# A recurrence of sixteen chains: two chains in turn over shifted periods, or one chain over one whole period

## The chip, the cores and the metric

One core of a Trainium2 chip. The metric is the time of one execution on the device in microseconds. The kernel before was run three times. One further execution was profiled; its span and its own time are given below.

## What is computed

One layer of a trunk for 128 context tokens and 512 latent tokens, width 2048, all in 32-bit floats. Its parts are a modulation, one input projection, three parallel token mixers, one output projection and a mixture of 16 experts. The change touches one of the mixers alone, the bidirectional recurrence (RWKV-7) of 16 heads of 64. The reference, cut to it:

```python
def wkv_scan(r, w, k, v, a, b, s0, reverse):
    def step(S, xs):
        r_t, w_t, k_t, v_t, a_t, b_t = xs
        sa = jnp.einsum('bhvk,bhk->bhv', S, a_t)
        S = S * w_t[:, :, None, :] + sa[..., None] * b_t[:, :, None, :] + v_t[..., None] * k_t[:, :, None, :]
        return S, jnp.einsum('bhvk,bhk->bhv', S, r_t)
    xs = tuple(jnp.swapaxes(t, 0, 1) for t in (r, w, k, v, a, b))
    s_T, o = lax.scan(step, s0.astype(jnp.float32), xs, reverse=reverse)
    return jnp.swapaxes(o, 0, 1), s_T

# one scan for each direction d, with its own decay and rate;
# the outputs of the two directions are added
o_d, s_d = wkv_scan(rf, decay_d, k_d, vf, -kk, kk * a_d, s0_d, rev)
o = outs[0] + outs[1]
```

The latent tokens start from a cached state, the context tokens from zero, and the final state of the context is an output of its own.

## The kernel before, in words

The program is a row of blocks, one after another: modulation, input projection, keys and attention, the recurrence (`block_rwkv`, lines 1112 to 1780), its output, output projection with experts, and a last block. Only `block_rwkv` is changed.

**Chains.** Heads are handled in pairs, 128 partitions for two heads; eight pairs and two directions make 16 chains, v = 0 to 15, pair v // 2 and direction v % 2. The 640 tokens are cut into 10 chunks of 64 (2 of context, 8 of latent). Within a chunk everything is matrix products; from chunk to chunk a state of 64 x 64 a head is carried. So each chain has parallel work, which is done for all its chunks at once, and a serial part of 10 chunks.

**The parallel work of a chain**, as jobs of PE into a ring of four PSUM banks (`rw_rot`, line 1491), each emptied by ACT or DVE. A job waits until the job four before it is emptied.
- w and a (four jobs) and s0: low-rank projections to decay and rate, and the turned start state. ACT empties them with tanh (lines 1579, 1581, 1583). After w, POOL shifts (line 1350), DVE makes the running sum (`scan`, line 1705), POOL makes products (`front`, lines 1358 to 1368), ACT exponentials (line 1613), DVE and POOL the scaled operands (lines 1710, 1717, 1722, 1372).
- sc, five jobs: the scores between tokens of a chunk, masked by DVE (line 1685).
- bk, three jobs, and vt, two jobs for each pair (in even periods): keys and values turned to rows (ACT, lines 1588, 1585).
- The inverse of a triangular matrix for each chunk. Blocks of 8 are sent over DRAM (SP, lines 1298 and 1301), solved by POOL (`solve`, lines 1395 to 1398), sent back (lines 1306, 1308) and laid out by `place` (line 1408). Then three levels (2, 3, 4), each with two x jobs and two d jobs; DVE empties x (line 1692) and d (line 1695) and transposes (`turn`, line 1677), which the next x job needs. The last d goes into `rw_tw` (line 1700), and `spread_own` (POOL, line 1415) fills its other half. `half0`, `half1` and `far` are copies of scores by ACT (line 1598).

**The serial part.** For each chunk three stages in this order (`stage`, lines 1503 to 1547 for PE):
- `pw`: five products with the values, the scores and the old state (rw_zo, rw_wu). It waits for the state of the chunk before and for the copy of its output. ACT copies the result to `rw_wsb` (line 1633).
- `u`: one product with the inverse; ACT copies to `rw_usb` (line 1641).
- `z`: two products; DVE makes the new state `rw_st` (line 1748, in the first chunk line 1746), and after it ACT copies the output to `rw_of` (line 1648).

**The order.** It is written out by hand in a list for each period u, `LINES[u]`. PE, ACT and DVE all walk through the same list and take what is theirs, in this order and no other. In a period u stand: the front jobs of chain u + 1, scores and bk of chain u, the levels of chain u - 1, and stages of chains. `spread_out` puts the stages, in equal measure, where the list says "slot". POOL and SP have orders of their own (loops from lines 1432 and 1314). In the kernel before the stages of a chain are shifted over parts of periods by `CUTS`: chunks 0 and 1 of chain v in the late part of period v + 1, chunks 2 to 4 in the early part of period v + 2, 5 and 6 in its late part, 7 to 9 in the early part of v + 3. `both` lets two chains take turns, stage by stage. There are 19 periods:

```python
return (spread_out(early(u), both(chain(u - 3, c, NCK), chain(u - 2, a, b)))
        + spread_out(late(u), both(chain(u - 2, b, c), chain(u - 1, 0, a))))
```

Of the kernel before, what the change touches and what calls it, by code (L numbers as in the profile page):

```python
# [20 lines left out]
P = 128  # L21
# [5 lines left out]
GRID_W, NAH, DH = 64, 8, 64  # L27
# [5 lines left out]
NCK = T // CK  # L33
# [1094 lines left out]
def block_rwkv(nc, z_d, kk_d, par_d, w2, a2, state, ident_d, o_raw_d, state_out, ffn_d, lb_d, tb_d, consts):  # L1128
# [9 lines left out]
    LEVELS = range(FIRST_LV, LAST_LV + 1)  # L1138
    CUTS = (2, 5, 7)
    STEPS = 2 * (SB - 2)  # L1140
# [7 lines left out]

    def early(u):

        w0, w1, a0, a1, s0 = front_jobs(u + 1) or [None] * 5
        now = u < NU
        sc = [("sc", b, u) if now else None for b in range(NCK // 2)]
        bk = [("bk", b, u) if now else None for b in range(2)]
        lv = {(kind, b, n): (kind, b, n, u - 1) if 1 <= u <= NU else None for kind in ("x", "d") for b in range(2) for n in LEVELS}
        turns = ["turn0", "turn1"] if 1 <= u <= NU else []
        items = [w0, a0, w1, a1, s0, "slot", sc[0], "scan", "slot", sc[1], "slot", sc[2], "slot", sc[3], "slot", sc[4], *turns, lv["x", 0, 2], "slot", lv["x", 1, 2], "slot", "removal",
                 lv["d", 0, 2], lv["d", 1, 2], "slot", "exp_in", lv["x", 0, 3], "slot", bk[0], lv["x", 1, 3], "exp_inv", "slot", "pad_b", lv["d", 0, 3], "slot", "half0",
                 lv["d", 1, 3], "exp_ex", "slot", "half1", "pad_k", lv["x", 0, 4], "slot", "decay", bk[1], lv["x", 1, 4], "slot", "far", lv["d", 0, 4], "slot", "pad_a", lv["d", 1, 4]]
        return kept_items(u, items)  # L1160

    def late(u):

        now = u < NU
        vt = [("vt", b, u) if now and u % 2 == 0 else None for b in range(2)]
        return kept_items(u, ["slot", ("bk", 2, u) if now else None, "slot", vt[0], "slot", vt[1], "slot"])

# [7 lines left out]
    def chain(v, i0, i1):  # L1175
        return [("seq", v, i, s) for i in range(i0, i1) for s in ("pw", "u", "z")] if 0 <= v < NU else []

    def both(one, two):
        return [s for pair in itertools.zip_longest(one, two) for s in pair if s is not None]

# [13 lines left out]
    def timeline(u):  # L1194

        a, b, c = CUTS
        return (spread_out(early(u), both(chain(u - 3, c, NCK), chain(u - 2, a, b)))
                + spread_out(late(u), both(chain(u - 2, b, c), chain(u - 1, 0, a))))

# [5 lines left out]

    LINES = [timeline(u) for u in range(NU + 3)]
    JOBS = front_jobs(0) + [i for line in LINES for i in line if not isinstance(i, str) and i[0] != "seq"]
# [7 lines left out]
    with ExitStack() as ctx:  # L1215
# [17 lines left out]
        bktok = sb("bktok", [P, NS, 2 * NCK, DH])  # L1233
        vtok = sb("vtok", [P, 2, NCK, DH])
        sc = sb("sc", [P, NS, NCK, 2, 2 * CK])
# [38 lines left out]
        def _(sp):  # L1274
# [10 lines left out]

            def store(p):
                for d in range(2):
                    sp.wait_ge(w_ev[d], p * NCK + NCP + 1)
                    sp.dma_start(state_out[d, bass.ds(2 * p, 2)].rearrange("o v k -> (o v) k"), fo[:, (2 * p + d) % 4, :]).then_inc(fo_out, 16)
                sp.wait_ge(osum_done, p + 2)  # L1290
                sp.dma_start(o_raw_d[bass.ds(p, 1)].rearrange("o p t -> p (o t)"), osum[:]).then_inc(o_out, 16)
# [49 lines left out]
        def _(pool):  # L1341
# [86 lines left out]
            for u in range(NU + 3):  # L1428
                if u + 1 < NU:
                    shift(u + 1)  # L1430
                if 1 <= u <= NU:
                    place(u - 1)
                if u + 1 < NU:
                    front(u + 1)
                    scaled_r(u + 1)
                if 1 <= u <= NU:
                    for b in range(2):
                        spread_own(u - 1, b)
                if u < NU:
                    solve(u)  # L1440
                if u + 1 < NU:
                    decay_pairs(u + 1)
                if u % 2 == 0 and 0 <= u // 2 - 2:
                    add_directions(u // 2 - 2)


        @block.tensor
        def _(pe):
# [64 lines left out]
            def stage(v, i, s):  # L1513
# [5 lines left out]
                wv, uv, fv, zv, ov = w[:, 0:DH], w[:, DH:2 * DH], w[:, 2 * DH:3 * DH], z[:, 0:DH], z[:, DH:2 * DH]  # L1519
                vk = vtok[:, v // 2 % 2, c, :]  # L1520
                if s == "pw":
# [41 lines left out]
        def _(act):  # L1563
# [3 lines left out]
            def empty(key):  # L1567
# [12 lines left out]
                elif kind == "a":  # L1580
                    a = nc.scalar.activation(ar[:, cols], bank[:, 0:HALF], ACT.Tanh, scale=0.5, bias=pp[:, 7 + u % 2:8 + u % 2])
                elif kind == "s0":
                    a = nc.scalar.copy(s0[:, u % 4, :], bank[:, 0:DH])
                elif kind == "vt":
                    a = nc.scalar.copy(chunks(vtok[:, u // 2 % 2], b).rearrange("p c k -> p (c k)"), bank[:, 0:BC * DH])
                elif kind == "bk":
                    m = min(8, 2 * NCK - 8 * b)
                    a = nc.scalar.copy(bktok[:, u % NS, 8 * b:8 * b + m, :].rearrange("p c k -> p (c k)"), bank[:, 0:m * DH])
# [1129 lines left out]
```

## Time and profile before

| what | us |
|---|---|
| median of three runs (3059.43 to 3063.23) | 3063.07 |
| the profiled execution, its own time | 3060.63 |
| its span | 3058.9 |
| PE busy, share of the span | 2697.3, 88% |
| DVE busy | 1367.3, 45% |
| ACT busy | 521.8, 17% |
| POOL busy | 453.7, 15% |
| first PE record of the recurrence | 1006.3 |
| its last output copy on ACT | 1526.1 |

The span is that of one execution in the hardware profile. Times of rows are microseconds from its start. PE is the matmul engine, PEld its loading of weights, SPq the queue of DMA issues. A product of two heads in 32-bit floats shows as four PE records. A row of the timeline merges records of the same kind; its second number is from the start of the first to the end of the last, and ends of matmuls overlap with what follows. PEclk is the granted clock of PE as a share of 2.4 GHz.

### The profile page before, as it was taken

The numbers are of one execution on the slowest core, as the hardware profiler recorded it, in microseconds if no ns is written. First come the engines' busy times: TensorE is split into PE (matmuls) and PEld (weight loads), VectorE is DVE, ScalarE is ACT, GpSimd is POOL, SyncE is SP. The second block draws the span as 40 slices with busy tenths as digits, with TensorE's granted clock in tenths as the row PEclk, the third lists the DMA queues.
The fourth block names the chain that finished last, engine by engine and source line by source line (L and its number), as shares of the span: only waits on it lengthen the run. The fifth ranks groups of instructions, "written<-read, shape, count | busy, mean of one in ns | idle before, by whom it ended". The sixth has DMA issues, their size and how long they took to land. (4 is left out here: it accounts for less than half of the span.)

```text
span 3058.9 us, 60845 instructions
## 1 busy us (share of the span) xinstructions
PE 2697.3 (88%) x25988; PEld 1525.7 (50%) x25988; DVE 1367.3 (45%) x2369; ACT 521.8 (17%) x1459; POOL 453.7 (15%) x639
## 2 busy tenths in 40 slices
PE   5799899999949489999867999999999999999992
PEld 1466676666637388888733444322333333333320
DVE  1658667676456355555371213432222333222323
ACT  1100000000045245555320211100000000000001
POOL 0100000000074455555120000000000000000000
PEclk8899999999979699999878999999999999999996
DMA  9576654646275311211078788899999999999997
GB/s 409 199 235 190 203 175 177 218 169 218 73 217 114 132 40 43 69 42 44 24 260 286 288 288 324 305 414 385 405 404 403 404 404 387 402 405 406 404 413 269
DMA packets 268517, 783.60 MB, mean 256 GB/s; under 512 B 99473, under 2 KB 163112, under 8 KB 199712
## 3 DMA queue, kind: packets, MB, share of 16 engines
q1 hardware_dynamic: 257104, 724.13, 63.0%
q0 software_dynamic: 10848, 56.51, 6.3%
q8 instruction: 152, 2.49, 0.3%
q14 instruction: 45, 0.37, 0.0%
q10 hardware_dynamic: 368, 0.10, 0.0%
HBM read 712.59 MB, written 68.08 MB: 255 GB/s over the span
## 5 line engine op out<-in xcount | busy, mean ns | idle before, releaser
L2207 PE MATMUL oe_ps<-experts_ring,tail_arena 128*32 128x512 f32 x4096 | 502.7, 606 | 43.7 <-DMA experts_ring<-in_w_up 43.7
L478 DVE SCALAR_TENSOR_TENSOR pj_macc<-pj_mring,head_cond_t,pj_macc 128x1024 f32<-128x1024 f32 x240 | 296.8, 1277 | 183.3 <-DMA pj_mring<-in_w_ada 183.3
L2207 PEld LDWEIGHTS oe_ps<-experts_ring,tail_arena 128*32 128x32 f32 x4096 | 149.3, 112 | 344.1 <-issue 343.1
L551 PE MATMUL pj_ps<-head_hT,head_ring_in 128*128 128x320 f32 x1104 | 312.4, 436 | 6.5 <-DVE head_hT L451 4.2
L2240 PE MATMUL oe_ps<-experts_ring,oe_hidt 128*32 128x512 f32 x2880 | 312.0, 592 | 0.0
L2215 PE MATMUL oe_ps<-experts_ring,tail_arena 128*32 128x512 f32 x2048 | 271.2, 597 | 0.0
L551 PEld LDWEIGHTS pj_ps<-head_hT,head_ring_in 128*128 128x128 f32 x1104 | 210.9, 191 | 96.7 <-DVE head_hT L451 6.6
L2544 DVE SCALAR_TENSOR_TENSOR oe_hid_s<-oe_hid_s,oe_gcol_s,oe_ps 128x512 f32<-128x512 f32 x16 | 12.0, 747 | 536.3 <-ACT oe_hid_s L2390 536.3
L2286 PE MATMUL oe_ps<-experts_ring,tail_arena 128*128 128x512 f32 x520 | 231.6, 602 | 15.8 <-DMA tail_arena<-scratch_o 15.8
L551 PE MATMUL pj_ps<-pj_t,pj_s 128*128 128x320 f32 x736 | 211.7, 442 | 6.6 <-DVE pj_t L457 6.6
L2240 PEld LDWEIGHTS oe_ps<-experts_ring,oe_hidt 128*32 128x32 f32 x2880 | 105.8, 110 | 203.2 <-issue 203.2
L551 PEld LDWEIGHTS pj_ps<-pj_t,pj_s 128*128 128x128 f32 x736 | 141.8, 194 | 73.3 <-issue 11.3
L2146 POOL DMA_INDIRECT scratch_ffn<-tail_arena,oe_tok x16 | 22.7, 1421 | 992.4 <-DVE tail_arena L2550 992.4
L2286 PEld LDWEIGHTS oe_ps<-experts_ring,tail_arena 128*128 128x128 f32 x520 | 98.5, 193 | 136.2 <-issue 119.2
L2215 PEld LDWEIGHTS oe_ps<-experts_ring,tail_arena 128*32 128x32 f32 x2048 | 75.8, 112 | 149.7 <-issue 149.7
L2455 DVE STREAM_TRANSPOSE tail_arena<-tail_arena 32x512 f32<-32x512 f32 x192 | 134.7, 702 | 23.1 <-DMA tail_arena<-scratch_h,oe_tok 16.6
L436 ACT COPY pj_stage<-pj_ps 128x320 f32<-128x320 f32 x23 | 9.8, 425 | 684.5 <-PE pj_ps L551 684.5
L2390 ACT ACTIVATE oe_hid_s<-oe_ps 128x512 f32<-128x512 f32 x16 | 9.6, 597 | 676.8 <-PE oe_ps L2215 676.8
L411 POOL DMA_DIRECT2D scratch_z<-pj_stage x19 | 14.0, 739 | 644.8 <-DVE pj_stage L496 644.8
L551 PE MATMUL pj_ps<-head_hT,pj_s 128*128 128x320 f32 x368 | 102.8, 432 | 0.0
L551 PE MATMUL pj_ps<-pj_t,head_ring_in 128*128 128x320 f32 x368 | 102.8, 432 | 0.0
L496 DVE TENSOR_TENSOR pj_stage<-pj_stage,pj_ps 128x320 f32<-128x320 f32 x161 | 75.3, 479 | 50.9 <-PE pj_ps L551 50.8
(411 smaller groups left out, 3861.1 us busy)
## 6 DMA issues: line engine op xcount, KB each, us to landing
experts_ring<-in_w_gate SPq DMA_DIRECT2D x128, 1024.0 KB, 23.6
experts_ring<-in_w_up SPq DMA_DIRECT2D x128, 1024.0 KB, 25.7
experts_ring<-in_w_down SPq DMA_DIRECT2D x128, 1024.0 KB, 22.2
experts_ring<-in_w_out SPq DMA_DIRECT2D x68, 1024.0 KB, 7.0
pj_mring<-in_w_ada SPq DMA_DIRECT2D x64, 1024.0 KB, 9.2
head_ring_in<-in_w_in SPq DMA_DIRECT2D x23, 2048.0 KB, 7.9
ada_ring<-in_w_ada SPq DMA_DIRECT2D x16, 2048.0 KB, 19.3
scratch_z<-pj_stage POOLq DMA_DIRECT2D x19, 640.0 KB, 8.2
```

The lines of the kernel that those rows point to most:

```text
L411: pool.dma_start(z_d[ZROW[b]:ZROW[b] + 2].rearrange("g p t -> p g t"), stage[:, slot]).then_inc(out_sem[slot], 16)
L436: nc.scalar.copy(c_part(b, 0, 0), bank("p1", b)[:, 0:TH]).then_inc(p1c, 1)
L478: a = nc.vector.scalar_tensor_tensor(acc, w, scalar, acc, ALU.mult, ALU.add)
L496: nc.vector.tensor_tensor(dst, one, bank(name, b)[:, 0:TH], ALU.add).then_inc(done, 1)
L551: mm = pe.matmul(bank(name, b)[:, 0:TH], a[:, k, :], h[:, k, :], start=(k == 0), stop=(k == KH - 1))
L2146: pool.indirect_dma_start(out=ffn_rows, out_offset=bass.IndirectOffsetOnAxis(ap=tok[:, e:e + 1], axis=0), in_=y, in_offset=None, compute_o ...
L2207: pe.matmul(ps[32 * i:32 * i + 32, bank, :], xe[:, k, GROUPS[i % 2]], w[:, kk * DE + 512 * (i // 2):kk * DE + 512 * (i // 2) + 512], start ...
L2215: mm = pe.matmul(ps[32 * i:32 * i + 32, GB + 2, :], xe[:, k, GROUPS[2]], w[:, kk * DE + 512 * (i % 2):kk * DE + 512 * (i % 2) + 512], star ...
L2240: mm = pe.matmul(ps[32 * i:32 * i + 32, DB + c, :], hidt[:, k, rows], w[:, col * 512:(col + 1) * 512], start=start, stop=stop)
L2286: mm = pe.matmul(ps[:, banks(t) + h, :], ot[:, t % 2, k, :], w[:, h * 512:(h + 1) * 512], start=(k == 0), stop=False)
L2455: tr = nc.vector.transpose(dst[32 * q:32 * q + 32, :, 32 * g:32 * g + 32], src[32 * g:32 * g + 32, :].rearrange("m (k p two) -> m k two p" ...
L2544: nc.vector.scalar_tensor_tensor(hid_s[:], hid_s[:], gcol_s[:], ps[:, GB + 1, :], ALU.mult, ALU.mult).then_inc(hid_done, 1)
```

## The change

Five things are edited, all in `block_rwkv`:
- `early` and `late` become one list, `plan`, with 18 slots. The chain u - 2 runs alone in it with all its 30 stages; `CUTS` and `both` go. There are 18 periods.
- In the list, bk 0 to 2 and vt 0 and 1 stand between the levels' jobs; before, bk 0 and 1 stood there, bk 2 and vt in the late part. `turn0` and `turn1` stand before sc 3 and before the first x job; sc 4 stands after that x job. Of the two d jobs of level 2 the second comes one slot later.
- `vtok` has three buffers in place of two.
- POOL runs `solve(u)` ahead of the two `spread_own(u - 1)`.
- SP waits, before it stores the states of a pair, until the stores of the pair before have landed.

```diff
-    CUTS = (2, 5, 7)
...
-    def early(u):
+    def plan(u):
 
         w0, w1, a0, a1, s0 = front_jobs(u + 1) or [None] * 5
         now = u < NU
         sc = [("sc", b, u) if now else None for b in range(NCK // 2)]
-        bk = [("bk", b, u) if now else None for b in range(2)]
+        bk = [("bk", b, u) if now else None for b in range(3)]
+        vt = [("vt", b, u) if now and u % 2 == 0 else None for b in range(2)]
         lv = {(kind, b, n): (kind, b, n, u - 1) if 1 <= u <= NU else None for kind in ("x", "d") for b in range(2) for n in LEVELS}
-        turns = ["turn0", "turn1"] if 1 <= u <= NU else []
-        items = [w0, a0, w1, a1, s0, "slot", sc[0], "scan", "slot", sc[1], "slot", sc[2], "slot", sc[3], "slot", sc[4], *turns, lv["x", 0, 2], "slot", lv["x", 1, 2], "slot", "removal",
-                 lv["d", 0, 2], lv["d", 1, 2], "slot", "exp_in", lv["x", 0, 3], "slot", bk[0], lv["x", 1, 3], "exp_inv", "slot", "pad_b", lv["d", 0, 3], "slot", "half0",
-                 lv["d", 1, 3], "exp_ex", "slot", "half1", "pad_k", lv["x", 0, 4], "slot", "decay", bk[1], lv["x", 1, 4], "slot", "far", lv["d", 0, 4], "slot", "pad_a", lv["d", 1, 4]]
+        turn0, turn1 = ("turn0", "turn1") if 1 <= u <= NU else (None, None)
+        items = [w0, a0, w1, a1, s0, "slot", sc[0], "scan", "slot", sc[1], "slot", sc[2], turn0, "slot", sc[3], turn1, "slot", lv["x", 0, 2], sc[4], "slot", lv["x", 1, 2], "slot", "removal",
+                 lv["d", 0, 2], bk[0], "slot", lv["d", 1, 2], "slot", "exp_in", lv["x", 0, 3], bk[1], "slot", lv["x", 1, 3], "exp_inv", "slot", "pad_b", lv["d", 0, 3], bk[2], "slot", "half0",
+                 lv["d", 1, 3], "exp_ex", "slot", "half1", "pad_k", lv["x", 0, 4], vt[0], "slot", "decay", lv["x", 1, 4], "slot", "far", lv["d", 0, 4], vt[1], "slot", "pad_a", lv["d", 1, 4], "slot", "slot"]
         return kept_items(u, items)
-
-    def late(u):
-
-        now = u < NU
-        vt = [("vt", b, u) if now and u % 2 == 0 else None for b in range(2)]
-        return kept_items(u, ["slot", ("bk", 2, u) if now else None, "slot", vt[0], "slot", vt[1], "slot"])
...
-    def both(one, two):
-        return [s for pair in itertools.zip_longest(one, two) for s in pair if s is not None]
...
     def timeline(u):
-
-        a, b, c = CUTS
-        return (spread_out(early(u), both(chain(u - 3, c, NCK), chain(u - 2, a, b)))
-                + spread_out(late(u), both(chain(u - 2, b, c), chain(u - 1, 0, a))))
+        return spread_out(plan(u), chain(u - 2, 0, NCK))
...
-    LINES = [timeline(u) for u in range(NU + 3)]
+    LINES = [timeline(u) for u in range(NU + 2)]
...
-        vtok = sb("vtok", [P, 2, NCK, DH])
+        vtok = sb("vtok", [P, 3, NCK, DH])
...
             def store(p):
+                if p:
+                    sp.wait_ge(fo_out, 32 * p + 1)
...
+                if u < NU:
+                    solve(u)
                 if 1 <= u <= NU:
                     for b in range(2):
                         spread_own(u - 1, b)
-                if u < NU:
-                    solve(u)
```

## Rows read from the trace of the kernel before

**Rows 1.** Busy time by stretch: the 13 full periods, then the stage's last part.

```profile
core 0: us, PE busy (x) PEld busy (x) DVE busy (x) ACT busy (x) POOL busy (x), PEclk, DMA share, GB/s
...
1077.06:1452.93 375.87, 342.28 (x9664) 321.00 (x9663) 210.50 (x491) 205.05 (x757) 209.14 (x331) 1.00 0.20 48
1452.93:1526.30 73.37, 62.27 (x1598) 55.91 (x1596) 24.23 (x69) 29.50 (x131) 9.93 (x22) 0.92 0.09 21
```

**Rows 2.** Timeline of DVE: start, time; the scans of periods 2 and 14.

```profile
1081.18 1.48 DVE L1705 TENSOR_TENSOR_SCAN rw_cs<-mixers_reset,rw_sg 128x640 f32<-128x640 f32 x1
...
1428.23 1.48 DVE L1705 TENSOR_TENSOR_SCAN rw_cs<-mixers_reset,rw_sg 128x640 f32<-128x640 f32 x1
```

**Rows 3.** Timeline of PE in period 8: start, time, product, records, idle before.

```profile
1256.66 1.04 PE L1462 MATMUL rw_rot<-rw_aq,rw_bk 64*64 64x128 f32 x16
1258.74 0.77 PE L1462 MATMUL rw_rot<-rw_tm,rw_near 64*64 64x32 f32 x20 [1.04 <-DVE rw_tm L1677]
...
1259.96 0.28 PE L1462 MATMUL rw_zo<-rw_vtok,rw_bktok 64*64 64x64 f32 x4
...
1260.54 0.72 PE L1462 MATMUL rw_rot<-rw_tm,rw_near 64*64 64x32 f32 x20
1261.10 0.31 PE L1462 MATMUL rw_wu<-rw_wsb,rw_tw 64*64 64x64 f32 x4
...
1264.07 1.10 PE L1462 MATMUL rw_rot<-rw_eye,rw_bk 64*64 64x64 f32 x32
```

**Rows 4.** Timeline of PE with chain 15 alone, chunks 6 to 8.

```profile
1510.28 0.33 PE L1462 MATMUL rw_zo<-rw_vtok,rw_bktok 64*64 64x64 f32 x4 [0.73 <-DVE rw_st L1748]
...
1511.27 0.33 PE L1462 MATMUL rw_wu<-rw_wsb,rw_tw 64*64 64x64 f32 x4 [0.18 <-ACT rw_wsb L1633]
1511.91 0.33 PE L1462 MATMUL rw_zo<-rw_usb,rw_bktok 64*64 64x64 f32 x4 [0.31 <-ACT rw_usb L1641]
...
1513.09 0.33 PE L1462 MATMUL rw_zo<-rw_vtok,rw_bktok 64*64 64x64 f32 x4 [0.73 <-DVE rw_st L1748]
...
1516.29 0.48 PE L1462 MATMUL rw_zo<-rw_vtok,rw_bktok 64*64 64x64 f32 x4 [0.72 <-DVE rw_st L1748]
...
1519.92 0.48 PE L1462 MATMUL rw_zo<-rw_vtok,rw_bktok 64*64 64x64 f32 x4 [0.72 <-DVE rw_st L1748]
```

**Rows 5.** Timeline of DVE in the same chunk: the new state.

```profile
1512.41 0.28 DVE L1748 SCALAR_TENSOR_TENSOR rw_st<-rw_zo,rw_ecp,rw_ste 128x64 f32<-128x64 f32 x1 [2.53 <-PE rw_zo L1462]
```

**Rows 6.** Timeline of ACT in the same chunk: the copy of the output.

```profile
1512.78 0.21 ACT L1648 COPY rw_of<-rw_zo 128x64 f32<-128x64 f32 x1 [0.92 <-DVE rw_st L1748]
```

**Rows 7.** Timeline of DVE: the first score job of period 9 emptied, then the scan.

```profile
1283.27 0.69 DVE L1685 TENSOR_TENSOR rw_sc<-rw_rot,mixers_mask 128x512 f32<-128x512 f32 x1 [3.24 <-PE rw_rot L1462]
1283.87 1.48 DVE L1705 TENSOR_TENSOR_SCAN rw_cs<-mixers_reset,rw_sg 128x640 f32<-128x640 f32 x1
```

**Rows 8.** Timeline of ACT: the front jobs of period 9 emptied, first and last of five.

```profile
1280.14 0.53 ACT L1579 ACTIVATE rw_sg<-rw_rot,rw_pp 128x320 f32<-128x320 f32 x1
...
1281.80 0.23 ACT L1583 COPY rw_s<-rw_rot 128x64 f32<-128x64 f32 x1
```

**Rows 9.** Busy time by short stretches, columns as in rows 1.

```profile
1060.00:1070.00 10.00, 8.61 (x192) 8.26 (x190) 6.78 (x14) 3.57 (x9) 4.88 (x5) 0.66 0.18 30
...
1505.00:1510.00 5.00, 4.01 (x94) 3.17 (x89) 0.85 (x3) 2.60 (x13) 0.00 (x0) 1.00 0.00 0
1510.00:1513.00 3.00, 1.58 (x32) 1.20 (x32) 0.28 (x1) 1.07 (x6) 0.00 (x0) 1.00 0.03 5
...
1516.00:1520.00 4.00, 2.59 (x34) 2.09 (x36) 0.28 (x1) 1.25 (x6) 0.00 (x0) 0.50 0.00 0
```

**Rows 10.** Timeline of PE: chain 0's first stage, then period 2's front jobs.

```profile
1072.29 0.31 PE L1462 MATMUL rw_zo<-rw_vtok,rw_bktok 64*64 64x64 f32 x4
...
1077.17 1.25 PE L1485 MATMUL rw_rot<-rw_xwa,rw_wa 64*64 64x320 f32 x14
```

**Rows 11.** Timeline of POOL in period 8: first `spread_own`, then the end of `solve`.

```profile
1267.63 0.40 POOL L1415 TENSOR_SCALAR rw_tw<-rw_tt,mixers_half 128x160 f32<-128x160 f32 x1 [2.34 <-DVE rw_tt L1695]
...
1276.06 0.23 POOL L1398 MEMSET rw_blk<- 16x80 f32 x1
```

More of the change, by code:

```diff
@@ L1438, in _ @@
                         spread_own(u - 1, b)
-                if u < NU:
-                    solve(u)
                 if u + 1 < NU:
                     decay_pairs(u + 1)
-                if u % 2 == 0 and 0 <= u // 2 - 2:
-                    add_directions(u // 2 - 2)
+                if u % 2 == 0 and u >= 4:
+                    add_directions((u - 4) // 2)
         @block.tensor
@@ L1519, in stage @@
                 wv, uv, fv, zv, ov = w[:, 0:DH], w[:, DH:2 * DH], w[:, 2 * DH:3 * DH], z[:, 0:DH], z[:, DH:2 * DH]
-                vk = vtok[:, v // 2 % 2, c, :]
+                vk = vtok[:, v // 2 % 3, c, :]
                 if s == "pw":
@@ L1584, in empty @@
                 elif kind == "vt":
-                    a = nc.scalar.copy(chunks(vtok[:, u // 2 % 2], b).rearrange("p c k -> p (c k)"), bank[:, 0:BC * DH])
+                    a = nc.scalar.copy(chunks(vtok[:, u // 2 % 3], b).rearrange("p c k -> p (c k)"), bank[:, 0:BC * DH])
                 elif kind == "bk":
```

## The prediction

> **What bounds the kernel now.** I read four views of the stage that the change touches, the recurrence. First the table by stretches: from 1077.06 to 1452.93 us the kernel runs 13 full periods, PE is busy for 342.28 of 375.87 us, and DVE, ACT and POOL are each near 56% [rows 1]. A period is the time between two scans on DVE, which come once in each: 12 intervals between the first and the last shown, (1428.23 - 1081.18) / 12 = 28.92 us [rows 2]. Then PE in order of time [rows 3]. PE takes its instructions in the order written, and its own queue stops at the first that has to wait: at 1258.74 it had been idle for 1.04 us for a transpose by DVE, with `pw` stages of two chains behind it. From start to start a `pw` (five groups of four records) takes 0.58 us, one x or d job (20 records) 0.56; a row's own time has a tail of 0.16 that overlaps the next, so an `sc` job is 0.88 and a full `bk` job 0.94. So PE's work in one period is: five sc, 4.4; twelve x and d, 6.7; three bk (2.5 jobs), 2.3; the two vt every second period, 1.2 / 2 = 0.6; the front jobs w, a, s0, 1.5 with their one wait; one chain, 9.1 (ten pw of 0.58, shorter at both ends, ten u of 0.12, ten z of 0.24). Sum 24.6, so PE stands still for 4.3 us of each period. The kernel is near PE's issue there, because two chains take turns and each covers the waits of the other.
>
> What a chain costs alone is to be seen at the stage's end, where only chain 15 is left [rows 4]. A chunk takes 1513.09 - 1510.28 = 2.81 us and holds 0.94 us of PE. The rest is three bare waits: pw start to u start 0.99, less 0.59 of issue, 0.40; u to z 0.64, less 0.12, 0.52; z to the next pw 1.18, less 0.24, 0.94, in which DVE makes the state and then ACT copies the output, one after the other [rows 5, 6].
>
> **The new order, step by step.** After the change a period holds one chain, 30 stages over 18 slots, so stages of the same chain stand next to each other with nothing between them. From `plan` and `spread_out` I wrote out an even period (P = pw, U = u, Z = z, with the chunk): front, P0 U0, sc0, scan, Z0 P1, sc1, U1, sc2, turn0, Z1 P2, sc3, turn1, U2 Z2, x and sc4, P3, x, U3 Z3, removal, d, bk, P4 U4, d, Z4, x, bk, P5 U5, x, Z5 P6, d, bk, U6, d, Z6 P7, x, vt, U7 Z7, x, P8, d, vt, U8 Z8, d, P9 U9 Z9.
>
> 1. *Bare waits.* Thirteen of the 29 steps from one stage to the next have no job between them: P to U at 0, 4, 5, 9 (4 x 0.40, and 0.11 more at 0, whose P is short) 1.7; U to Z at 2, 3, 7, 8, 9, 2.6; Z to P at 0, 1, 5, 6, 3.8. At Z7 and Z8 one job of 0.56 covers only part of 0.94: 0.8. Elsewhere the jobs hide the wait. 24.6 + 8.9 = 33.5 us.
> 2. *The queues of DVE and ACT.* The state after Z0 now stands behind the emptying of sc0 and the scan on DVE [rows 7]. sc0 is emptied 1.08 after its start, the scan comes 0.60 later and holds DVE for 1.40, so P1 starts 2.58 after the end of Z0 instead of 0.94: +1.6. In the old order sc1 and sc2 ran on PE meanwhile; now they stand behind P1. The same with sc2's emptying and turn0 ahead of the state of Z1: +0.6. U0 needs a copy that stands behind four tanh of 0.42 and the s0 copy on ACT [rows 8], from 1280.14 to the end of that copy's issue: +0.4. d and x emptied ahead of Z5, and half0, exp_ex and d13 ahead of Z6: +0.5. The vt copies and `far` ahead of U7 and U8: +0.4 even, +0.2 odd. Sum 3.5.
>
> A period is then 33.5 + 3.5 = 37.0 us at the full clock, 8.1 more than 28.9. Bounds: 33.5 if the queues never bite; above, the clock.
>
> 3. *PE's clock.* While two chains took turns without jobs (1505 to 1510) the granted clock stayed 1.00, that is 2.4 GHz, with PE busy for 4.01 of 5.00 us; with one chain it was busy for 1.58 of 3.00 and the clock then fell to 0.50, 1.2 GHz [rows 9]. A chunk there took 1519.92 - 1516.29 = 3.63 us [rows 4]. The new period has the same thin stretch from Z0 to P1 (about 1.2 us of work in 4.7), another at its end, and 24.6 / 37.0 = 66% of work over all. The nearest stretch for that share is 1060 to 1070, jobs alone with gaps, at 0.66 [rows 9]. I take some 5.5 us of each period at the lower clock, where progress is 2.81 / 3.63 = 77% of full: 1.3, somewhat more where jobs lie dense: +1.7. Ends: 0, and half of the period, +8. Forecast 38.7 us a period.
>
> Of this clock the Trainium skill (TensorE: Matmul & The Clock Gate, section on HAM oscillation) says that it falls over long idle gaps between groups of matmuls; no gap of the new order is of that sort, and by that rule the 1.7 is 0. The tail rows speak against it: the clock fell with waits under 1.1 us.
>
> 4. *Start and end.* Chain 0 no longer starts in period 1: PE is done with that period's jobs at 1072.3, and the next front jobs, now at 1077.1, follow at once [rows 10]: -4.6. The first period is as before. The last three hold less. From 1452.93 to 1526.30 they took 73.4 us [rows 1]. Now: chain 13 with the jobs of score period 15, without front, scan and tanh: 33. Chain 14 with x and d alone: ten chunks of 2.81 less the last Z to P and the short ends are 26.8; jobs longer than their wait and queues +1.8; half of it at the lower clock +3.4: 32. Chain 15 alone, all at the lower clock after its first chunks, 26.8 x 3.63 / 2.81 = 34.5. Sum 99.5, so +26.1. One period fewer in the list saves nothing by itself: what it held is here.
>
> 5. *POOL, SP, the third vtok buffer: 0.* `solve` runs ahead of the two `spread_own`. Before, the first of these waited 2.34 us for DVE and began at 1267.63, and `solve` behind them ended at 1276.3 [rows 11]. Now it uses that wait and goes ahead of their 2 us, so it ends some 4 us earlier. So the copy back and `place` come earlier, and `turn0` finds its input; behind it `spread_own` ends some 3 us later, but its readers are the first u two periods on and the next `place`. If that cover were gone, U0 would wait those 3 us in each period. On SP the state stores wait for the pair before, which was stored two periods earlier; behind them queue the loads for the next pair, which then start no later than the copy back lets them. Vtok only needs space. That `turn0` moves ahead of sc3 removes the 1.04 us wait of rows 3; it is counted, since no such wait stands in the 37.0.
>
> **Sum.** 13 x (38.7 - 28.9) = 127.4; end +26.1; start -4.6: +149 us. The profiled execution took 3060.63, its span 3058.9; that gives 3209.6. The median of the runs is 2.4 us higher, so I say 3212.
>
> **Rivals.**
> A, the forecast: 50%. Its own range is 3190 to 3245.
> B, the clock holds but in the last period (33.5 + 3.5 = 37.0): 13 x 8.1 = 105.3, end 32.5 + 28.6 + 34.5 - 73.4 = +22.2, start -4.6: +123, 3186. For it: the two chains at 1.00. Against it: the tail. 31%. It is also what the skill's rule gives.
> C, the clock stays low for half of the time or more (period about 45, from PE work of twice the length in half of it; end +30): 13 x 16.1 + 30 - 4.6 = +235, 3298. 8%.
> D, the queues hardly bite and the clock holds (33.5): 13 x 4.6 + 17 - 4.6 = +72, 3135. 8%. My order by hand could be too strict where ACT and DVE overlap.
> E, faster: PE goes on with the jobs behind a waiting stage, so that the bare waits cost nothing and a period is PE's 24.6: 13 x -4.3 = -56, end 24 + 27 + 34.5 - 73.4 = +12, start -4.6: -48, 3015. Its place is PE's queue at each of the 13 bare waits; it decides once waits and queues together are under 4.3 us a period, against 12.4 in my sum. The row at 1258.74 speaks against it: two ready chains stood behind a waiting job. 2%.
> That nothing changes would need a chain as long as before; 1%. The order is written out, so it can't fail to take effect.
>
> **Range and chances.** About 0.2% (6 us) is what can be told from no change. From 3155 to 3262 lie A and B nearly whole, and the edges of C and D: 8 in 10. Faster 0.02, same 0.01, slower 0.97.
>
> **What would show it.** The scans about 38 us apart (A), 37 (B), 33.5 (D). PE idle some 2 us or more between the output copy of chunk 0 and pw of chunk 1, and DVE's scan between them. Bare waits of 0.4, 0.5 and 0.9 at the places named. The granted clock under 1.00 for some us of most periods (A) or only at the end (B). The stage's last chain alone for about 34 us at 0.5. Front jobs of period 2 at about 1072.5. Wrong would be: scans under 32 us apart, PE records of a job between a stage and its wait, or `turn0` waiting for POOL.

## The result, and the profile after

| what | before | after |
|---|---|---|
| median, us | 3063.15 (4 runs) | 3258.39 (4 runs, 3252.03 to 3263.7) |
| ratio | | 1.064 [1.0619, 1.066] |
| span of the profiled execution | 3058.9 | 3250.3 |
| mean interval of scans, periods 2 to 14 | 28.92 | 41.39 |

The change costs 195 us. The prediction said 149, so 3212. The result is inside the stated range (3155 to 3262), but only 3.6 us below its upper edge, and above rival A's own range, which ended at 3245.

**Where the time went.** First DVE in order of time, the scans of periods 2 and 14, which answer to [rows 2]:

```profile
1074.85 1.48 DVE L1695 TENSOR_TENSOR_SCAN rw_cs<-mixers_reset,rw_sg 128x640 f32<-128x640 f32 x1
...
1571.52 1.48 DVE L1695 TENSOR_TENSOR_SCAN rw_cs<-mixers_reset,rw_sg 128x640 f32<-128x640 f32 x1
```

(1571.52 - 1074.85) / 12 = 41.39 us. Then the table by stretches, as in [rows 1]: the full periods, from there to the end of period 15 (the last with score jobs), then chain 14 and chain 15:

```profile
core 0: us, PE busy (x) PEld busy (x) DVE busy (x) ACT busy (x) POOL busy (x), PEclk, DMA share, GB/s
1074.85:1571.52 496.67, 385.29 (x8976) 353.10 (x8976) 200.12 (x457) 194.19 (x708) 193.32 (x307) 0.88 0.14 35
1571.52:1645.90 74.38, 59.17 (x1414) 55.63 (x1414) 27.98 (x69) 25.97 (x100) 22.57 (x42) 0.85 0.10 21
1645.90:1686.00 40.10, 34.03 (x554) 30.95 (x555) 9.14 (x27) 8.45 (x39) 2.29 (x3) 0.50 0.03 11
1686.00:1721.60 35.60, 24.38 (x312) 19.00 (x310) 2.49 (x9) 8.76 (x40) 0.00 (x0) 0.50 0.01 3
```

PE was busy for 91% of the full periods, now 78%. The granted clock was 1.00 in their mean, now it is 0.88: 24% of the time at 0.50. The last two chains run at 0.50 throughout.

Period 2's front jobs start at 1069.0 (before 1077.1), period 15's first stage at 1607.56 (before about 1452.9), and the stage ends at 1721.6 (before 1526.3). The stage itself started 1.4 us earlier, and what follows it was 3.9 shorter. So the difference of the spans splits into: ahead of the stage -1.4; its first periods -6.6; 13 periods, 538.5 - 375.9 = +162.7; its end, 114.0 - 73.4 = +40.6; behind it -3.9. Sum +191.4, which is 3250.3 - 3058.9.

**Inside a period.** PE in order of time from the start of the chain in one period (to be held against [rows 3]; the value in brackets is PE's idle time and what ended it):

```profile
1318.98 0.33 PE L1452 MATMUL rw_rot<-rw_eye,rw_sin 64*64 64x64 f32 x4
1319.20 0.33 PE L1452 MATMUL rw_zo<-rw_vtok,rw_bktok 64*64 64x64 f32 x4
...
1320.45 0.33 PE L1452 MATMUL rw_wu<-rw_wsb,rw_tw 64*64 64x64 f32 x4 [0.68 <-ACT rw_wsb L1623]
1320.67 1.09 PE L1452 MATMUL rw_rot<-rw_aq,rw_bk 64*64 64x128 f32 x16
1321.56 0.31 PE L1452 MATMUL rw_zo<-rw_usb,rw_bktok 64*64 64x64 f32 x4
1321.68 0.31 PE L1452 MATMUL rw_zo<-rw_sc,rw_usb 64*64 64x64 f32 x4
1324.39 0.48 PE L1452 MATMUL rw_zo<-rw_vtok,rw_bktok 64*64 64x64 f32 x4 [2.40 <-DVE rw_st L1736]
...
1325.48 1.94 PE L1452 MATMUL rw_rot<-rw_aq,rw_bk 64*64 64x128 f32 x16
...
1327.40 1.94 PE L1452 MATMUL rw_rot<-rw_aq,rw_bk 64*64 64x128 f32 x16
...
1331.62 1.07 PE L1452 MATMUL rw_rot<-rw_aq,rw_bk 64*64 64x128 f32 x16
...
1333.10 0.33 PE L1452 MATMUL rw_zo<-rw_usb,rw_bktok 64*64 64x64 f32 x4 [0.30 <-ACT rw_usb L1631]
```

This is the order written out in the prediction: P0 U0, sc0, Z0, a wait, P1, sc1, and so on. Behind the wait of 2.40 us, small products take 0.48 where they took 0.33, and an sc job 1.94 where it takes 1.07 at the full clock. DVE at the same place shows what the 2.40 was:

```profile
1321.80 0.69 DVE L1675 TENSOR_TENSOR rw_sc<-rw_rot,mixers_mask 128x512 f32<-128x512 f32 x1 [5.21 <-PE rw_rot L1452]
1322.40 1.48 DVE L1695 TENSOR_TENSOR_SCAN rw_cs<-mixers_reset,rw_sg 128x640 f32<-128x640 f32 x1
1323.80 0.20 DVE L1736 TENSOR_TENSOR rw_st<-rw_zo,rw_ecp 128x64 f32<-128x64 f32 x1
```

Z0 was issued by 1321.8, yet its state is made at 1323.80, behind the emptying of sc0 and the scan. The clock by short stretches: the first third of this period, its two other thirds, and two stretches of another period:

```profile
1318.40:1331.00 12.60, 8.31 (x119) 7.42 (x113) 4.00 (x7) 3.50 (x13) 7.08 (x8) 0.73 0.01 2
1331.00:1344.00 13.00, 11.48 (x340) 10.94 (x341) 5.70 (x14) 4.90 (x20) 1.53 (x1) 1.00 0.19 32
1344.00:1357.50 13.50, 10.17 (x304) 9.37 (x300) 6.82 (x18) 7.67 (x27) 8.37 (x17) 1.00 0.13 38
...
1497.00:1507.00 10.00, 8.94 (x274) 8.52 (x272) 5.71 (x14) 3.36 (x13) 0.00 (x0) 1.00 0.21 37
...
1517.00:1533.13 16.13, 13.81 (x237) 11.57 (x234) 3.80 (x11) 6.39 (x23) 3.40 (x5) 0.67 0.32 110
```

The low clock comes at the start of each period, and in some even periods a second time near the end. Even periods hold two vt jobs more than odd ones, so each is to be held against its own kind. These are the intervals of scans after two even periods, 6 and 8, the first of them with a second low stretch:

```profile
1238.50:1284.05 45.55, 36.73 (x768) 33.59 (x768) 16.84 (x41) 16.73 (x60) 16.92 (x26) 0.78 0.19 54
...
1322.40:1363.15 40.75, 31.31 (x768) 28.82 (x768) 16.64 (x41) 16.52 (x60) 16.99 (x26) 0.92 0.21 59
```

Four of the six even intervals are like the first (45.06 to 45.80 us, clock 0.77 to 0.81), two like the second; the odd ones take 38.35 to 39.35 us at 0.91 to 0.96.

### The profile page after: what moved, and what is told of

The parts are those of the page before. It is cut to its first block and busy times, and to the rows that moved or that the text cites. A ratio compares the mean times of both kernels' runs of the same rounds, so it can differ in the third digit from the quotient of the medians.

```text
span 3250.3 us, 60881 instructions
## 1 busy us (share of the span) xinstructions
PE 2797.6 (86%) x25988; PEld 1618.6 (50%) x25988; DVE 1373.2 (42%) x2369; ACT 525.3 (16%) x1459; POOL 452.9 (14%) x639
## 5 line engine op out<-in xcount | busy, mean ns | idle before, releaser
L2197 PE MATMUL oe_ps<-experts_ring,tail_arena 128*32 128x512 f32 x4096 | 502.6, 605 | 40.1 <-DMA experts_ring<-in_w_up 40.1
L551 PEld LDWEIGHTS pj_ps<-pj_t,pj_s 128*128 128x128 f32 x736 | 141.3, 193 | 72.7 <-issue 10.4
L1675 DVE TENSOR_TENSOR rw_sc<-rw_rot,mixers_mask 128x512 f32<-128x512 f32 x80 | 55.2, 690 | 186.7 <-PE rw_rot L1452 186.7
L1452 PE MATMUL rw_rot<-rw_aq,rw_bk 64*64 64x128 f32 x1280 | 106.9, 319 | 3.2 <-DVE rw_aq L1712 3.2
L1452 PE MATMUL rw_zo<-rw_vtok,rw_bktok 64*64 64x64 f32 x576 | 51.1, 254 | 66.6 <-DVE rw_st L1736 33.7
```

The costliest lines, as they stand in the source:

```text
L551: mm = pe.matmul(bank(name, b)[:, 0:TH], a[:, k, :], h[:, k, :], start=(k == 0), stop=(k == KH - 1))
L1452: mm = pe.matmul(out[rows], lhs[rows], rhs[rows], start=start, stop=stop, **kw)
L1675: nc.vector.tensor_tensor(sc[:, u % NS, 2 * b:2 * b + 2].rearrange("p c i n -> p (c i) n"), bank.rearrange("p (i n) -> p i n", n=2 * CK), ...
L2197: pe.matmul(ps[32 * i:32 * i + 32, bank, :], xe[:, k, GROUPS[i % 2]], w[:, kk * DE + 512 * (i // 2):kk * DE + 512 * (i // 2) + 512], start ...
```

## The experiments

Three theories stood to be told apart: the waits and queues of a lone chain (steps 1 and 2); PE's clock (step 3); and that the new list, POOL's order or SP's wait had a part in it (step 5 put them at nothing).

**Two chains with the new list (two_new).** After, with two chains in turn put back; list, POOL, SP and vtok stay new.

```diff
-        return spread_out(plan(u), chain(u - 2, 0, NCK))
+        return spread_out(plan(u), both(chain(u - 3, 5, NCK), chain(u - 2, 0, 5)))
...
-    LINES = [timeline(u) for u in range(NU + 2)]
+    LINES = [timeline(u) for u in range(NU + 3)]
```

> The kernel after with its new list, order on POOL, wait on SP and third vtok buffer, but two chains in turn: chunks 5 to 9 of chain u - 3 with chunks 0 to 4 of chain u - 2. Theory 1 (the time went into the waits of a chain that runs alone, into the queues of DVE and ACT it stands behind, and into PE's clock): a period of 28 to 29 us, granted clock 1.00 from period 3 on, 3035 to 3065 us, since the 1.04 us wait for the transpose goes and period 1 holds no chain. Rival 1 (the new list or the order on POOL and SP costs it, not the lone chain): 3150 us or more.

Measured: 3041.49 us (3039.24 to 3046.85), 0.9947 [0.9929, 0.9966] of the kernel before, and 217 less than after. Its full periods by stretch, 331.35 / 12 = 27.61 us each, with PE busy for 92% and the clock at 1.00:

```profile
1077.02:1408.37 331.35, 306.22 (x8856) 291.43 (x8854) 201.58 (x453) 182.41 (x692) 195.61 (x307) 1.00 0.21 53
```

The whole loss comes from one edit, one chain for two. The rest of the change, the third vtok buffer with it, gains.

**One chain with the old list (one_old).** Before, with a lone chain over early and late lists; POOL and SP old; three vtok buffers for space.

```diff
-        return (spread_out(early(u), both(chain(u - 3, c, NCK), chain(u - 2, a, b)))
-                + spread_out(late(u), both(chain(u - 2, b, c), chain(u - 1, 0, a))))
+        return spread_out(early(u) + late(u), chain(u - 2, 0, NCK))
```

> The kernel before with its own list of jobs and its order on POOL and SP, but one chain alone in each period, chunks 0 to 9 of chain u - 2 spread over all its slots (and the third vtok buffer, which that needs). Theory 1: as slow as the kernel after or slower by up to 1 us a period, since the transpose is waited for again: 3250 to 3290 us, a period of 41 to 43 us. Rival 1: the old list keeps the time near that of before, 3063 to 3100 us.

Measured: 3279.0 us, 1.0703 [1.0655, 1.0752]. The four runs were 3265, 3266, 3292 and 3292 us. The profiled one is the 3292, with scans 44.52 us apart, above the 41 to 43 expected. A lone chain loses in the old list too, by the medians some 21 us more than in the new one; held against either pair of runs it is 7 or 34.

**Two chains with the old list (two_old).** The fourth corner: as one_old, but with `both(chain(u - 3, 5, NCK), chain(u - 2, 0, 5))` and 19 periods.

> The fourth corner of two lists by one or two chains: the list of jobs of the kernel before, but two chains in turn, halves of 5 chunks over whole periods as in two_new. Theory 1: near the kernel before, 3045 to 3065 us, so that the step from two chains to one costs over 200 us with either list. Rival 1: over 3100.

Measured: 3072.01 us (3070.26 to 3073.84), 1.0045 [1.003, 1.0061], period 29.81, 7 us above what was expected. Beside the kernel before it has halves of five chunks in place of `CUTS` and a third vtok buffer, and the 13 us lie in these. The four corners:

| us | two chains | one chain | difference |
|---|---|---|---|
| old list | 3072.0 | 3279.0 | +207 |
| new list | 3041.5 | 3258.4 | +217 |
| difference | -30.5 | -21 | |

One chain costs over 200 us with either list; the 10 us between the two differences are less than the spread of one_old.

**Cover for the bare waits (after_fill).** After, with matmuls whose result nobody reads wherever a stage follows a stage: one after pw, two after u, three after z, and more in the first chunks of periods with a scan. Work is added and none left out.

```diff
+            def fill(line, n, item):
+
+                work = [x for x in line[n + 1:] if not isinstance(x, str)]
+                if not work or work[0][0] != "seq":
+                    return
+                v, i, s = item[1:]
+                busy = "scan" in line
+                count = {"pw": 3 if busy and i == 0 else 1, "u": 2, "z": (9 if i == 0 else 5 if i == 1 else 3) if busy else 3}[s]
+                for _ in range(count):
+                    heads(wu[:, 1 - v % 2, 256:384], eye[:], mask[:, 0, :], True, True)
```

> The kernel after with matmuls whose result nobody reads put into the bare waits of the lone chain (64x64 by 128 columns: one pair after a pw, two after a u, three after a z where the next item is the same chain's, nine after z of chunk 0 and five after z of chunk 1 where the scan is in the period). They keep PE busy and add no wait at the full clock. Theory 1: the granted clock is 0.97 or more from period 3 to 15, the period falls from 41.4 to 37 to 38.5 us, the last two chains from 75 to 57 to 62, time 3175 to 3215 us; what is then left above the kernel before, 110 to 150 us, is waits and queues. Rival 2 (the lower clock lies inside waits and costs little): the clock rises, the time stays above 3240. Rival 3 (the clock is nearly all of it): under 3110.

Measured: 3187.78 us (3185.18 to 3189.04), 1.0419 [1.0398, 1.0439], which is 70.6 less than after although PE does more. By stretch, the 12 intervals of scans and then the rest of the stage:

```profile
1078.46:1532.08 453.62, 427.24 (x10714) 386.19 (x10713) 199.74 (x457) 193.89 (x708) 194.43 (x307) 1.00 0.16 39
1532.08:1656.00 123.92, 115.98 (x2857) 102.15 (x2853) 39.66 (x105) 43.10 (x179) 24.98 (x45) 1.00 0.08 17
```

The clock is 1.00 in both, to the end, where the lone chain ran at 0.50 before. A period takes 453.62 / 12 = 37.80 us. From the scan of period 14 to the last output it is 123.6 us; after has 149.8, before 97.9. So the fillers take 12 x 3.59 = 43 us from the periods and 26 from the end. That is what the low clock cost, or somewhat less, since fillers can also delay a stage. At the widest wait they did not: P1 starts 1270.47 - 1267.87 = 2.60 us after Z0 in after_fill, and 2.59 in after.

By kind of period the gain fits the clock. Even intervals are 38.45 us in after_fill but for the first (38.97), and were 40.75 without the second low stretch, 45.06 to 45.80 with it; odd ones are 37.06 and were 38.35 to 39.35. Of the 43 us, 28 are won in the four even intervals with a second low stretch. The waits and queues themselves are left: 3187.8 - 3063.2 = 125 us.

**The scan out of the state's way (after_scan, fill_scan).** "scan" goes behind sc1, once in after and once in after_fill (there with three fillers after Z0 in place of nine).

```diff
-... "slot", sc[0], "scan", "slot", sc[1], "slot", sc[2], ...
+... "slot", sc[0], "slot", sc[1], "scan", "slot", sc[2], ...
```

> The kernel after with one word of the list moved: the scan stands behind the second score job instead of the first, so that the state of chunk 0 does not stand behind it on DVE. Theory 1: the wait before pw of chunk 1 falls from 2.4 to about 1.0, of which some comes back at the second score job's emptying and the state of chunk 1; 0.8 to 1.6 us a period less, 3235 to 3248 us. Rival 4 (that wait ends by something else, or the clock takes it all back): 3254 to 3262.

> The run after_fill with its scan behind the second score job, so that the price of the scan's place is read at the full clock. Theory 1: the wait before pw of chunk 1 falls from 2.6 to about 1.0 and no more than 0.5 us comes back; 1.1 to 1.6 us a period, 3167 to 3175 us in place of 3188. Rival 4: it all comes back at the second score job and the state of chunk 1, 3184 to 3190.

Measured: after_scan 3244.3 us (3236.43 to 3264.51), 14 less than after, with intervals that overlap. fill_scan 3183.41 us (3181.84 to 3185.66), 1.0409, only 4.4 less than after_fill, with ratios whose intervals overlap, and not the 13 to 21 expected; a period falls from 37.80 to 37.40. So rival 4 was right for fill_scan. PE of after_scan, in the execution of 3264.51 us, shows why:

```profile
1210.01 0.33 PE L1452 MATMUL rw_zo<-rw_vtok,rw_bktok 64*64 64x64 f32 x4 [1.02 <-DVE rw_st L1736]
...
1212.60 0.31 PE L1452 MATMUL rw_zo<-rw_sc,rw_usb 64*64 64x64 f32 x4
1215.21 0.33 PE L1452 MATMUL rw_wu<-rw_eye,rw_fs 64*64 64x64 f32 x4 [2.31 <-DVE rw_fs L1734]
```

The wait ahead of P1 fell from 2.40 to 1.02, and the one ahead of P2 rose from 1.12 to 2.31: the state of chunk 1 (rw_fs, the context's final state) is now the one behind the scan. At neither of the two places tried does enough work of PE stand between the state behind the scan and the stage that needs it.

**POOL and SP alone (before_pool).** Before, with `solve` ahead of `spread_own` and SP's wait.

```diff
+                if p:
+                    sp.wait_ge(fo_out, 32 * p + 1)
...
+                if u < NU:
+                    solve(u)
                 if 1 <= u <= NU:
                     for b in range(2):
                         spread_own(u - 1, b)
-                if u < NU:
-                    solve(u)
```

> The kernel before with two parts of the change alone: POOL solves ahead of the two spread_own, and SP waits before a pair's state stores for the stores of the pair before. Theory 1: nothing, 3054 to 3066 us (beside a kernel before of 3057 to 3063), a ratio of 0.998 to 1.002; solve ends some 4 us earlier in its period, and nothing waits for it. Rival 1: part of the slowdown sits here, over 3070.

Measured: 3062.33 us, 1.0011 [1.0002, 1.002]: some 3 us, nothing beside 195. Step 5 holds in the old order.

**The same with two chains and the new list (two_new_pool).** two_new, with `solve` behind `spread_own` again.

```diff
-                if u < NU:
-                    solve(u)
                 if 1 <= u <= NU:
                     for b in range(2):
                         spread_own(u - 1, b)
+                if u < NU:
+                    solve(u)
```

> The run two_new with POOL's old order, both spread_own ahead of solve. With the lone chains gone, this is the version that might beat all. Theory 1 (nobody waits for solve): 3038 to 3043 us, the same as two_new. Rival (solve first costs a little, as the ratio 1.0011 of before_pool hints): 3 us less, 3036 to 3039.

Measured: 3051.96 us (12 runs, 3044.29 to 3056.33), 0.9976 [0.9965, 0.9987], period 28.17, some 10 us above two_new, with intervals of the two ratios that just meet. Theory and rival both had it lower. POOL's old order costs nothing in the old list and some 10 us in the new one. Why is not shown. `turn0` stands earlier in the new list and needs what comes back from `solve`, but in these 12 periods DVE waits for that only four times, 2.0 us in all. PE's waits inside parallel jobs for which the profile names no releaser rose more, from 0.8 us in two_new to 10.4 in 14 places.

**The turns' place alone (before_turn).** Before, with turn0, turn1 and sc4 placed as in the new list.

```diff
-... sc[2], "slot", sc[3], "slot", sc[4], *turns, lv["x", 0, 2], "slot", ...
+... sc[2], turn0, "slot", sc[3], turn1, "slot", lv["x", 0, 2], sc[4], "slot", ...
```

> The kernel before with one other part of the change alone: turn0 and turn1 before score job 3 and before the first x job, score job 4 behind that x job. Chains, slots, POOL and SP as before. Theory 1: the 1.04 us wait for the transpose goes from each of 15 periods, and part of it comes back as a later state: 5 to 15 us less than the kernel before. Rival 5 (what follows waits instead, so nothing is won): within 4 us of before.

Measured: 3055.82 us, 0.9987 [0.9977, 0.9996], some 4 us less and not the 5 to 15 expected. Moving the turns takes only part of the wait away: over 12 periods PE waits for the transpose 24 times, 18.5 us in all, in before, and 23 times, 13.5 us in all, here. The profiled execution was the longest of the 11 (3068.32 us); its scans came 29.4 us apart in the mean, no closer than in before, with one interval of 34.7 and the clock at 0.96:

```profile
1082.74:1435.47 352.73, 326.63 (x8914) 308.88 (x8910) 197.59 (x455) 189.35 (x699) 192.47 (x305) 0.96 0.20 50
```

**A job in nearly every gap (one_dense), and the same with fillers (dense_fill).** One chain, but the list written out so that a job stands in 25 of its 29 gaps (23 in odd periods, which have no vt). Its core:

```diff
+        items = [w0, c(0, "pw"), a0, c(0, "u"), w1, c(0, "z"), a1, sc[0], c(1, "pw"), s0, c(1, "u"), sc[1], c(1, "z"), turn0, turn1, sc[2],
+                 c(2, "pw"), x[0][0], c(2, "u"), x[0][1], c(2, "z"), "scan", sc[3], c(3, "pw"), d[0][0], c(3, "u"), d[0][1], c(3, "z"), sc[4],
...
+                 c(7, "pw"), d[2][0], c(7, "u"), d[2][1], c(7, "z"), "decay", "far", vt[0], c(8, "pw"), c(8, "u"), c(8, "z"), "pad_a", vt[1],
+                 c(9, "pw"), c(9, "u"), c(9, "z")]
```

> The kernel after with the same jobs and one chain a period, but the list written out so that a job of PE stands in 25 of the 29 waits of the chain, and the long work of DVE and ACT (scan, removal, pads, exponentials) right behind a z. Theory 1 (bare waits and queues): a period of 29.5 to 31.5 us at a clock of 1.00, the last two chains as slow as in the kernel after (75 us): 3095 to 3125 us. Rival 6 (a lone chain costs 37 us a period wherever the jobs stand): over 3170.

> The run one_dense with unread matmuls in the waits that still have no job, as in after_fill. It tells how much of that run's 35.9 us a period was the clock (granted 0.91 there) and how much the waits on ACT and DVE that my placing made, of which the trace shows 0.7 to 1.3 us behind far and the value copies. Theory 1: clock 0.98 or more, 33 to 34.5 us a period, the last two chains 57 to 62 us in place of 75, 3140 to 3155 us. Rival 2: the waits are all, over 3175.

Measured: one_dense 3187.08 us (3184 to 3190.54), 1.0421 [1.0405, 1.0437], period 35.89, clock 0.90; over 60 us above what was expected, and where rival 6 had it. dense_fill 3135.32 us (3130.21 to 3142.0), 1.0261 [1.0244, 1.0278]; period 33.51 and clock 1.00 as expected, the time 5 us under the expected range. Their full periods by stretch, one_dense and then dense_fill:

```profile
1086.82:1517.54 430.72, 378.79 (x8981) 332.43 (x8978) 202.00 (x457) 194.22 (x708) 189.54 (x305) 0.90 0.16 41
```

```profile
1084.80:1486.96 402.16, 369.39 (x9413) 327.07 (x9410) 201.59 (x457) 192.74 (x708) 190.19 (x305) 1.00 0.18 44
```

So some 50 us of one_dense was the clock again. What is left, 33.51 us a period for the 29.5 to 31.5 expected, lies at least in part in queues. This is ACT of one_dense, and then PE where it waits:

```profile
1321.40 1.01 ACT L1596 ACTIVATE rw_far<-rw_sc,mixers_half 128x320 f32<-128x320 f32 x2
1322.33 0.40 ACT L1583 COPY rw_vtok<-rw_rot 128x320 f32<-128x320 f32 x1
1322.88 0.19 ACT L1631 COPY rw_wsb<-rw_wu 128x64 f32<-128x64 f32 x1
```

```profile
1323.13 0.33 PE L1460 MATMUL rw_wu<-rw_wsb,rw_tw 64*64 64x64 f32 x4 [1.31 <-ACT rw_wsb L1631]
```

A copy of 0.19 us, for which PE waits, stands behind 1.4 us of copies of far scores and value tokens. Jobs in the gaps hide the round trip but bring their own emptying into the chain's queue.

**A try for more (two_best).** two_new, with the front jobs split by slots, the scan behind a later stage, and fillers in the last period.

```diff
-        items = [w0, a0, w1, a1, s0, "slot", sc[0], "scan", "slot", sc[1], "slot", ...
+        items = [w0, a0, "slot", w1, a1, "slot", s0, sc[0], "slot", "scan", sc[1], "slot", ...
```

> The run two_new with its front jobs set apart by two slots, the scan behind the z of the older chain, and unread matmuls in the waits of the last period, where chain 15 is alone. Theory 1: of the two waits that are left in its period, 1.28 for tanh and 1.15 for the state, most goes: 26.2 to 27.2 us a period in place of 27.6, and 3 us less at the end: 3020 to 3037 us. Rival: the period is bound by PE's issue already, 3036 to 3041.

Measured: 3046.56 us (3040.54 to 3048.27), 0.9952 [0.9938, 0.9965], period 27.99. No gain over two_new. It came out above both its expectation and the rival's. The two waits it aimed at are these, on PE in two_new. The first comes in every second period (1.12 to 1.35 us), the second in each, mostly 0.87 us long:

```profile
1266.31 0.33 PE L1455 MATMUL rw_rot<-rw_eye,rw_sin 64*64 64x64 f32 x4 [1.28 <-ACT rw_sg L1572]
...
1272.04 0.33 PE L1455 MATMUL rw_zo<-rw_vtok,rw_bktok 64*64 64x64 f32 x4 [1.15 <-DVE rw_st L1741]
```

In two_best the wait for tanh is gone and the one for the state is down from 11.3 to 4.9 us over 12 periods. In their place PE waits 3.4 us for rw_wsb (0 in two_new) and 8.0 us in 31 places ahead of writes to rw_zo for which the profile names no releaser (1.3 in 7 places in two_new). two_new has the lowest median of all kernels run here, 0.5% under the kernel before.

## Why the prediction was right, and where it was wrong

**Steps 1 and 2, bare waits and queues: right.** They gave 37.0 us a period at the full clock; after_fill has 37.80 at a clock of 1.00. The parts show in the rows. The forecast counted a wait from the end of issue, and the profile's brackets count it some 0.21 less, since the tail of the last row is in between. P to U of chunk 0 shows 0.68, so 0.89 by the forecast's count (forecast 0.40 + 0.11, and 0.4 of queue); the bare wait ahead of a z shows the 0.30 that it showed as 0.31 in [rows 4]; and P1 starts 1324.39 - 1321.80 = 2.59 us after the end of Z0 (forecast 2.58). Over 12 periods of after the brackets sum to 110.6 us in 176 places, 9.2 us a period, or 12.3 by the forecast's count; the forecast had 8.9 + 3.5 = 12.4. Rival B, 3186 us, adds start and end to this sum, with chain 15 at the low clock. after_fill measured 3187.8; that they agree so closely is partly luck. The periods took 13 x 0.8 = 10 us more than B had, and the last three chains 90.1 us in place of 95.6, since chain 15 ran at the full clock there (27.5 us, not 34.5). One item was priced as if it stood alone: the scan. It does hold the state for the time said, but without it another state would stand behind it. Taking it from Z0 and putting it one job later won 0.4 us a period, not 1.6.

**Step 3, the clock: this is what failed.** "I take some 5.5 us of each period at the lower clock, where progress is 2.81 / 3.63 = 77% of full: 1.3, somewhat more where jobs lie dense: +1.7." The mechanism was right, the term was too small by half, in both of its factors. The clock was low for 24% of 41.39 = 9.9 us of a period in the mean. This mean is of two kinds. With the length times twice what the clock lacks to 1.00, it is some 3 to 7 us in eight of the twelve intervals, about what was forecast, and 17 to 21 us in the four even ones with a second long stretch. The prediction named the thin stretch at the period's end, but did not price what follows once the clock is low there. And the low clock cost 41.39 - 37.80 = 3.6 us, 36% of its time, not 23%. The 77% came from a lone chain [rows 4], where most of the time is round trips that PE's clock does not touch. In the periods sc and bk jobs run in the low stretch, and an sc job takes 1.94 us for 1.07. The allowance for dense jobs, 0.4, was too little. The 1060 to 1070 stretch of [rows 9] was also taken as one with a 66% share of work, but PE is busy for 8.61 of its 10.00 us. It shows what dense jobs pay: a full bk job took 1.95 us at 1063.90 and 1.13 at 1069.41. Over 13 periods it is 3.6 x 13 = 47 us where 22 were allowed.

**Step 4, start and end.** The start was forecast at -4.6 and came out at -6.6: the front jobs do follow at once. It missed one wait, in period 2 alone, where U0 of chain 0 stood 1.39 us for POOL's `spread_own`, now behind `solve`:

```profile
1072.88 0.33 PE L1452 MATMUL rw_wu<-rw_wsb,rw_tw 64*64 64x64 f32 x4 [1.39 <-POOL rw_tw L1405]
```

The end was forecast at 33 + 32 + 34.5 = 99.5 us and took 38.3 + 40.1 + 35.6 = 114.0. The last term was right: a chain alone at 0.50 was to be read in [rows 4]. The two others failed by the clock again; with fillers, at a clock of 1.00, they took 33.8 and 28.8 us, close to the 32.5 and 28.6 that B has for them. Chain 13 was given 0.5 us for the clock, and its stretch shows a clock of 0.79. Chain 14 with x and d jobs beside it was taken as low for half of the time; it was low for all of it. With fillers the time from the scan of period 14 to the end is 26 us shorter, of which 24 lie in these last three chains, 114.0 for 90.1 (70.6 in all, less 13 x 3.6, is the same).

**Step 5, POOL, SP and vtok at nothing: right** for the kernel before (1.0011) and for the size that matters here. It is not so in two_new, where POOL's order is worth some 10 us.

**The sum.** Forecast +105 for waits and queues in the periods, +22 for the clock there, +26 for the end, -5 for the start. Measured: 8.88 x 13 = +115, 3.6 x 13 = +47, +41, -7. Of the 47 us that the stage took over the forecast, 25 are the clock in the periods, 15 the end, 10 the waits; the start gives 2 back.

**The rivals.** B was the right account of everything but the clock, and C had the clock's share too high (about 24% and not half). D fell: queues bite, by 37.8 - 33.5 = 4.3 us at the full clock, if the 33.5 of work and bare waits is right. E fell: PE stands at each bare wait with jobs written behind it. The Trainium skill's rule (TensorE: Matmul & The Clock Gate, section on HAM oscillation), by which long idle gaps between groups of matmuls bring the clock down, does not account for this kernel: the longest wait that came in every period was some 2.4 us, and while the last chain ran at 0.50 its waits were no longer than in [rows 4]. The same page has a section on a second HAM failure mode, in which frequent short idle times between groups of matmuls let the clock swing; it tells it of a kernel that cycles through PSUM banks. The traces here agree with short idle times as the cause (0.88 in the periods of after, 1.00 once fillers stand in the short waits), and the prediction had weighed only the first.

**Why so much was lost at all.** The kernel before has a serial chain whose every step is a round trip PE, ACT, PE or PE, DVE, PE of 0.4 to 0.94 us. With two chains in turn one's stage is the other's cover, and the clock stays up. With one, only jobs can be cover. In the change's list 13 of the 29 gaps have none; in one_dense only 4 have none, and there the jobs' own emptying stands in the queues that the chain runs through. The best arrangement of one chain found here, dense_fill, is still 94 us above two chains with the same jobs.

## What to carry to other kernels

In this kernel two serial chains in turn were worth over 200 us against a chain in one piece, since the stages of each cover the round trips of the other. Where a list is in order on every engine, price a lone chain as its round trips plus whatever stands ahead of its small copies on ACT and DVE. And price TensorE's clock by the jobs that run in the low stretch, with the factor of those jobs (1.8 for the sc jobs here, 1.3 for a lone chain), and over every thin stretch of the list, not the first alone; matmuls that nobody reads, put into the waits, tell in one run what the clock costs.

## What the runs showed of the hardware

The granted clock came out of step with the busy share of whole periods. In stretches of over 300 us: 0.80 with PE busy for 80% (one_old), 0.88 with 78% (after), 0.90 with 88% (one_dense), 1.00 with 91% (before) and 1.00 with 94% (after_fill). Matmuls take longer at the low clock, so the share itself rises with it. Within after the clock fell at the waits of a period's start and, in four of twelve periods, for a second long stretch near its end, in period 12 behind waits of 0.45 and 0.87 us with jobs between them. It did not come back at once when PE had work again: in that period it was 0.50 from 1520 to 1524, where PE was busy for all of the 4.00 us.

Adding work made the kernel faster. The fillers of after_fill put 1738 PE records into 12 periods (10714 in place of 8976), and the periods became 3.6 us shorter each; the whole kernel gained 70.6 us. In dense_fill 432 records (9413 for 8981) did the same, for some 50 us.

The low clock also set the rhythm. The same list, that of an even period, took 40.75 us in one period and 45.55 in another of the same execution, as the clock fell once or twice in it; with fillers the intervals are 37.06 and 38.45 in turn, which fits the value jobs (vt) of every second period. And one_old, at a clock of 0.80, spread over 27 us in its runs where after_fill spread over 4.
